# A hybrid mLSTM and sparse attention layer on one core: x laid out columns first by the host, bias tables from the host, three weight pairs multiplied part by part, two key transposes moved

## The reference

```
h = x * rsqrt(mean(x * x) + eps) * norm_gain          # first RMSNorm
proj = h @ w_in                                       # 4096 x 15416
ck, cv, sk, sv, wk, wv, a_q, gates, m_q, m_k, ... = split(proj)
k_cmp = compress(blocks of ck + cmp_k_pos), v_cmp likewise    # 15 blocks of 32 tokens
logits = q . k * scale + rel_bias[bucket(t - s)]      # compressed, selected and window keys
o = sigmoid(gates) combination of three softmax branches, times silu(a_z)
y_m = chunkwise mLSTM of conv(m_q, m_k), normed, gated
out = rmsnorm(x + concat(y_m, y_a) @ w_out)
```

## Time and profile before

| what | value |
|---|---|
| time, median of 3 runs (lowest to highest) | 1852.78 us (1850.45 to 1853.86) |
| the profiled execution: its own time, its span | 1850.58 us, 1848.8 us |
| TensorE busy, share of the span | 1820.6 us, 98% |
| VectorE, ScalarE, GpSimd busy | 62%, 45%, 4% |
| bytes moved, mean rate | 345.62 MB, 187 GB/s |
| chain that ended last, TensorE's share | 95% |

### The profile page before, as it was taken

How to read it: one execution, slowest core, us unless ns; L and a number is a source line. 1 busy time by engine, 2 the same in 40 slices (tenths; PEclk the granted TensorE clock), 3 DMA queues, 4 the chain that set the end, 5 groups by cost and what they waited for, 6 DMA issues and landing times.

```text
span 1848.8 us, 24131 instructions
## 1 busy us (share of the span) xinstructions
PE 1820.6 (98%) x8488; PEld 1511.8 (82%) x8488; DVE 1141.1 (62%) x1461; ACT 828.7 (45%) x1120; POOL 77.1 (4%) x54
## 2 busy tenths in 40 slices
PE   7999999999999999999999999999999999999997
PEld 6878888888888888888888888888888888888886
DVE  4544644467676676876666666756675775455554
ACT  5534444444454444434444444444443544444443
POOL 0000000000101010010000000000000000000000
PEclk9999999999999999999999999999999999999999
DMA  7676555544545444445555556555655566666664
GB/s 266 184 198 208 194 190 192 193 160 149 181 147 171 158 159 160 152 167 172 193 193 188 177 193 193 185 181 194 192 184 181 172 217 237 205 205 204 205 203 172
DMA packets 100266, 345.62 MB, mean 187 GB/s; under 512 B 10932, under 2 KB 16052, under 8 KB 100052
## 3 DMA queue, kind: packets, MB, share of 16 engines
q1 hardware_dynamic: 93448, 332.68, 54.1%
q10 hardware_dynamic: 6736, 11.77, 2.6%
HBM read 337.07 MB, written 7.33 MB: 186 GB/s over the span
## 4 chain that ended last, share of the span: by engine, by line
PE 95%; DMA 2%; ACT 1%; DVE 1%; issue 0%; SPq 0%; POOL 0%; ACTq 0%; DVEq 0%; POOLq 0%
PE acc_a L441 15%; PE acc_b L441 15%; PE acc_a L443 14%; PE acc_a L442 14%; PE acc_b L443 14%; PE acc_b L442 14%; PE bank_v L448 1%; DMA w_raw<-in_w_all 1%; PE bank_z L689 1%; DMA toe_dram<-toe_row 1%; PE bank_x L443 1%; PE bank_x L442 1%; PE bank_x L441 0%; ACT w_split L843 0%; PE bank_v L449 0%
## 5 line engine op out<-in xcount | busy, mean ns | idle before, releaser
L1206 DVE TENSOR_TENSOR w_split<-w_raw,w_split 128x1024 fp32r<-128x1024 f32 x620 | 777.1, 1255 | 599.2 <-ACT w_split L843 596.1
L843 ACT ACTIVATE w_split<-w_raw 128x1024 fp32r<-128x1024 f32 x620 | 655.3, 1059 | 848.9 <-PE acc_a L443 415.2
L441 PE MATMUL acc_a<-w_split,lhs_hi 128*128 128x512 f32 x1216 | 483.3, 397 | 3.2 <-DVE lhs_lo L1275 3.2
L441 PE MATMUL acc_b<-w_split,lhs_hi 128*128 128x512 f32 x1216 | 479.4, 394 | 0.3 <-issue 0.3
L443 PE MATMUL acc_a<-w_split,lhs_lo 128*128 128x512 f32 x1216 | 474.7, 390 | 0.0
L442 PE MATMUL acc_a<-w_split,lhs_hi 128*128 128x512 f32 x1216 | 474.6, 390 | 0.0
L443 PE MATMUL acc_b<-w_split,lhs_lo 128*128 128x512 f32 x1216 | 473.7, 390 | 0.0
L442 PE MATMUL acc_b<-w_split,lhs_hi 128*128 128x512 f32 x1216 | 473.6, 389 | 0.0
L441 PEld LDWEIGHTS acc_a<-w_split,lhs_hi 128*128 128x128 f32 x1216 | 229.0, 188 | 49.2 <-DVE lhs_lo L1275 2.4
L443 PEld LDWEIGHTS acc_a<-w_split,lhs_lo 128*128 128x128 f32 x1216 | 228.7, 188 | 48.7
L443 PEld LDWEIGHTS acc_b<-w_split,lhs_lo 128*128 128x128 f32 x1216 | 228.3, 188 | 48.1
(11 more groups left out here) (274 smaller groups left out, 927.0 us busy)
## 6 DMA issues: line engine op xcount, KB each, us to landing
w_raw<-in_w_all SPq DMA_DIRECT2D x616, 512.0 KB
wide<-in_x SPq DMA_DIRECT2D x8, 512.0 KB, 10.1
xres<-in_x ACTq DMA_DIRECT2D x8, 512.0 KB, 4.3
out_y<-wide SPq DMA_DIRECT2D x8, 512.0 KB, 3.2
toe_dram<-toe_row ACTq DMA_DIRECT2D x4, 766.0 KB, 10.2
toe<-toe_dram ACTq DMA_DIRECT2D x4, 512.0 KB, 4.6
gain_f<-in_final_norm_gain ACTq DMA_DIRECT2D x1, 2048.0 KB, 14.2
w_raw<-in_w_all SPq DMA_DIRECT2D x4, 224.0 KB
```

The lines of the kernel that those rows point to most:

```text
L441: pe.matmul(dst, a[0], b[0], start=start, stop=False)
L843: act.activation(w_hi[:, cols], w_raw[:, cols], ACT.Copy).then_inc(hi_done, 1)
L1206: dve.tensor_tensor(w_lo[:, cols], w_raw[:, cols], w_hi[:, cols].bitcast(F32), ALU.subtract).then_inc(lo_done, 1)
```

## The change

The host adds three arrays and drops the small ones: `x_cols_first` (x transposed, 128 partitions x (32 gains + 32 x 256 values)), `consts` (identity, masks, gains, positions, conv weights, second compressor layer, gate biases and the finished compressed bias table, 128x1318) and `toe_bias` (the finished causal bias table, 128x4096).

- SP loads `x_cols_first` in eight pieces into the memory of `lhs_lo` (`gained_x`), the first with the gains at its head, in between the first weight pairs. Weight pair 0 comes in two halves. Behind pair 7 comes `consts`, and behind each of pairs 8 to 15 an eighth of x in natural layout, which only the squares need.
- ScalarE and VectorE split x from SBUF (`first_hi`, `first_lo`), VectorE in place; the gains' transpose, `x_t`, `prepare_rows` and `prepare_bias` are gone from TensorE. The eight squares move from every second slot of block 0 to its last eight slots.
- TensorE first multiplies a tile of ones eight times (`WARM`), then pairs 0, 1 and 2 part by part (`early_pair`): hi x hi as soon as the hi parts are there, then lo of x, then lo of w.
- `copies_out` and `first_bias` are gone; ScalarE loads `toe` straight from `toe_bias` after block 0, and later groups likewise.
- T_CK moves from slot 1 to slot 6 of block 1, T_CV from the border to behind the first wide pair of block 2. T_SK moves from slot 1 to slot 2 of block 3. The parts of these transposes on ScalarE and VectorE move with them.

```diff
+WARM = 8
+XT_CHUNKS = ((0, 2), (2, 4), (4, 6), (6, 8), (8, 12), (12, 16), (16, 24), (24, 32))
...
+        gain_start = (nc.sbuf_base + 31) // 32 * 32
+        lhs_lo_start = gain_start + 4 * KT_IN
+        sb("lhs_lo_space", KT_IN + KT_IN * T)
+        gained_x = nc.alloc_sbuf_tensor_at("gained_x", [P, KT_IN + KT_IN * T], F32,
+                                           offset=gain_start)[:, :]
+        gain_t, x_t = gained_x[:, 0:KT_IN], gained_x[:, KT_IN:].rearrange("p (k t) -> p k t", t=T)
+        lhs_lo = nc.alloc_sbuf_tensor_at("lhs_lo", [P, KT_IN * T], F32R, offset=lhs_lo_start)[
+            :, :].rearrange("p (k t) -> p k t", t=T)
...
+            def fetch_xt(i):
+                if i == 0:
+                    sp.dma_start(gained_x[:, 0:KT_IN + 2 * T], x_cols_first[:, 0:KT_IN + 2 * T]
+                                 ).then_inc(xt_in[i], 16)
+                    return
+                ks = slice(*XT_CHUNKS[i])
+                sp.dma_start(x_t[:, ks, :], x_cols_first[:, KT_IN:].rearrange(
+                    "p (k t) -> p k t", t=T)[:, ks, :]).then_inc(xt_in[i], 16)
...
-            fetch_x(0)
-            fetch_first(0)
-            fetch_x(1)
+            fetch_xt(0)
+            sp.dma_start(slot_of(0, 0, 1), w_all[0:P, 0:BW]).then_inc(half_in, 16)
+            sp.dma_start(slot_of(0, 1, 1), w_all[0:P, BW:2 * BW]
+                         ).then_inc(w_loaded[0], LOADED)
+            fetch_xt(1)
             fetch_first(1)
-            fetch_x(2)
+            fetch_xt(2)
             fetch_first(2)
-            fetch_x(3)
+            fetch_xt(3)
             fetch_first(3)
-            for i in range(4, 8):
+            fetch_xt(4)
+            fetch_xt(5)
+            fetch_first(4)
+            fetch_xt(6)
+            fetch_first(5, 6)
+            fetch_xt(7)
+            fetch_first(7)
+            sp.dma_start(c128[:, :], consts).then_inc(consts_in, 16)
+            for i in range(8):
+                fetch_first(8 + i)
                 fetch_x(i)
...
-            def x_t(c):
-
-                if c % 2 == 0:
-                    pe.wait_ge(x_in[c // 2], 16)
-                if c >= 2:
-                    pe.wait_ge(ht_lo, c - 1)
+            pe.wait_ge(warm_set, 1)
+            for _ in range(WARM):
+                pe.matmul(bv[:, :], warm[:, 0:P], warm[:, :], start=True, stop=True)
...
+                def products(k, i, j):
+                    for t in range(TT):
+                        last = pe.matmul(acc[0][t][:, :], a[k][t][i], w[k][j],
+                                         start=(c, k, i, j) == (0, 0, 0, 0), stop=False)
+                    return last
+                if c == 0:
+                    pe.wait_ge(first_x_hi, 1)
+                    pe.wait_ge(half_hi, 1)
+                    products(0, 0, 0)
+                    pe.wait_ge(ht_lo, 1)
+                    products(0, 1, 0)
+                    pe.wait_ge(half_lo, 1)
+                    products(0, 0, 1)
+                    pe.wait_ge(hi_done, 1)
+                    products(1, 0, 0)
+                    products(1, 1, 0)
+                    pe.wait_ge(lo_done, 1)
+                    products(1, 0, 1).then_inc(pe_used, 1)
+                    return
+                pe.wait_ge(ht_hi, c)
+                pe.wait_ge(hi_done, c + 1)
...
+            for c in range(LOOKAHEAD):
+                early_pair(c)
+            for c in range(LOOKAHEAD, PAIRS):
                 pe.wait_ge(ht_lo, c + 1)
                 pair(0, c, 0)
-                if c + 2 < PAIRS:
-                    x_t(c + 2)
-                if c == 6:
-                    prepare_rows()
-                if c in (8, 9):
-                    prepare_bias(c - 8)
-            pe.wait_ge(pre_dve, 2)
-            pe.wait_ge(pre_act, 2)
-            stream(1, 1, {1: [lambda: transpose_stage(T_CK, 0)]})
+            pe.wait_ge(consts_in, 16)
+            stream(1, 1, {6: [lambda: transpose_stage(T_CK, 0)]})
...
-            transpose_stage(T_CV, 1)
...
+                if c == 1:
+                    transpose_stage(T_CV, 1)
...
-            stream(3, 1, {1: [key_block], 2: [hidden_t], 7: [compressed, running_sum],
+            stream(3, 1, {2: [key_block, hidden_t], 7: [compressed, running_sum],
                           10: [a_rows], 13: [m_columns]})
...
+            def first_hi(c):
+                for i, (first, _) in enumerate(XT_CHUNKS):
+                    if first == 2 * c:
+                        act.wait_ge(xt_in[i], 16)
+                for kk in (2 * c, 2 * c + 1):
+                    last = act.activation(lhs_hi[:, kk, :], x_t[:, kk, :], ACT.Copy,
+                                          scale=gain_t[:, kk:kk + 1])
+                last.then_inc(ht_hi, 1)
...
+            act.wait_ge(half_in, 16)
+            act.activation(w_hi[:, 0:BW], w_raw[:, 0:BW], ACT.Copy).then_inc(half_hi, 1)
+            act.wait_ge(w_loaded[0], LOADED)
+            act.activation(w_hi[:, BW:2 * BW], w_raw[:, BW:2 * BW], ACT.Copy).then_inc(hi_done, 1)
+            first_hi(1)
...
                 slot(0, c)
-                if c == 6:
-                    act.wait_ge(consts_in, 16 * N_CONST)
-                    act.activation(hot_r[:, :], hot_up, ACT.Copy)
-                    act.activation(rb_split[:, 0:HEADS_A], rb[:, :], ACT.Copy
-                                   ).then_inc(rb_hi_done, 1)
-                if c == 8:
-                    act.wait_ge(pre_pe, 2)
-                    act.activation(gain_mix[:, KT_IN // 2:KT_IN], bx[:, 192:192 + KT_IN // 2],
-                                   ACT.Copy)
-                    act.activation(pos_t[:, :], bx[:, 0:2 * CMP_L], ACT.Copy)
-                    act.activation(conv_w[:, :], bx[:, 128:192], ACT.Copy).then_inc(pre_act, 1)
-                if c % 2 == 1:
-                    t, i = divmod(c // 2, 4)
+                if c >= PAIRS - 8:
+                    i, t = divmod(c - (PAIRS - 8), 2)
                     act.wait_ge(x_in[2 * i], 16)
                     act.wait_ge(x_in[2 * i + 1], 16)
                     link(act.activation(junk[:, :], x_nat[:, t, i * 1024:(i + 1) * 1024],
                                         ACT.Square, accum_out=ss8[:, t, i:i + 1]))
-            act.activation(spare[:, 1:2], gain_t[:, 0:1], ACT.Copy).then_inc(pre_act, 1)
+            act.wait_ge(consts_in, 16)
+            act.activation(spare[:, 2:3], gain_t[:, 0:1], ACT.Copy).then_inc(pre_act, 1)
             act.wait_ge(pre_pool, 1)
             take(0, 0, stage[:, 0, :])
...
-            def copies_out(i):
-
-                act.wait_ge(pre_dve, 1)
...
-                act.wait_ge(toe_out, 4 * 16)
...
+            act.dma_start(toe[:, :], toe_bias[:, 0:HPG * T]).then_inc(toe_in, 16)
...
-            stream(1, {2: [lambda: transposed(T_CK, lambda i: by_group(cin[0][0])[:, 2 * i:2 * i + 2, :])],
-                       3: [lambda: copies_out(0)], 5: [positions_hi], 6: [lambda: copies_out(1)],
-                       9: [lambda: copies_out(2)], 12: [lambda: copies_out(3)],
-                       15: [first_bias]})
+            stream(1, {7: [lambda: transposed(T_CK, lambda i: by_group(cin[0][0])[:, 2 * i:2 * i + 2, :])],
+                       10: [positions_hi]})
...
-                if j == 1:
+                if j == 4:
...
+            dve.wait_ge(xt_in[0], 16)
+            for kk in range(2):
+                last = dve.tensor_scalar(lhs_hi[:, kk, :], x_t[:, kk, :], gain_t[:, kk:kk + 1],
+                                         None, ALU.mult)
+            last.then_inc(first_x_hi, 1)
+            first_lo(0)
+            dve.wait_ge(half_hi, 1)
+            dve.tensor_tensor(w_lo[:, 0:BW], w_raw[:, 0:BW], w_hi[:, 0:BW].bitcast(F32),
+                              ALU.subtract).then_inc(half_lo, 1)
+            dve.wait_ge(hi_done, 1)
+            dve.tensor_tensor(w_lo[:, BW:2 * BW], w_raw[:, BW:2 * BW],
+                              w_hi[:, BW:2 * BW].bitcast(F32), ALU.subtract).then_inc(lo_done, 1)
+            first_lo(1)
...
+        x=x, x_cols_first=np.concatenate(
+            [norm_gain.reshape(KT_IN, P).T,
+             x[0].T.reshape(KT_IN, P, T).transpose(1, 0, 2).reshape(P, KT_IN * T)], axis=1),
+        w_all=weight_stream(*map(np.asarray, (w_in, w_out, cmp_k_w1, cmp_v_w1))), final_norm_gain=final_norm_gain,
+        consts=constants(mlstm_norm_gain, cmp_k_pos, cmp_v_pos, w_conv, cmp_k_w2, cmp_v_w2,
+                         b_igate, b_fgate, rel_bias),
```

More of the change, by code:

```diff
@@ L521, in prepare_bias @@
-            def prepare_bias(t):
-                pe.wait_ge(rb_lo_done, 1)
-                for n in range(N_CMP):
-                    start = 255 + t * P - (CMP_S * n + CMP_L - 1)
-                    last = pe.matmul((bz, bv)[t][:, 2 * n * HEADS_A:2 * (n + 1) * HEADS_A],
-                                     hot_r[:, start:start + P], rb_split[:, :],
-                                     start=True, stop=True)
-                last.then_inc(pre_pe, 1)
-            pe.wait_ge(first_in, 32)
```

(24 more changed lines are left out.)

294 lines of the change are left out of this document (116 added, 178 removed).

## The result

The changed kernel takes 1867.1 us (median of 4 runs, 1866.73 to 1868.38), the kernel before 1851.62 (4 runs, 1850.14 to 1853.86). The ratio is 1.0076, with a 95% interval of 1.0063 to 1.009: 15.5 us slower. The forecast was 1829.

A forecast was written before the change was run, and what follows sets the result against it. TensorE, busy nearly the whole span, was taken as the bound; savings of 16.6 us in block 0 and 7.0 us at the transposes sum to 23.6, so 1852.8 - 23.6 = 1829 us, range 1824 to 1836.

The forecast's parts named there:

- Nothing gives it back later: the rest is paced by TensorE: After the early savings, the remaining execution: claimed no loss there, so the summed saving of 23.6 us stays whole.
- a slow stream: Block 0 loads at 225 GB/s: block 0 ends at 85, 15 us later than before, total 1861 us; chance 2%.
- The signs that I named for being wrong: Block 0 ending before 51 or after 57 us, or a new wait appearing in blocks 1 to 3.
- Block 0: Block 0 was to end at 53.5 instead of 70.1 us, saving 16.6 us.
- The rest: Key transposes behind block 0: waits and lowered clock go, saving 0.2 + 3.7 + 1.7 + 1.4 = 7.0 us.
- First wide matmul: Start of block 0: TensorE can start at about 5.8 us instead of 10.26.
- The early products and the warming: Start of block 0: part-by-part products and warm matmuls worth almost nothing; without the stream as bound, up to 4.5 + 1.5 us.
- either edit alone would do most of it: T_CV's 3.7 us wait: removing toe copies and waiting load, or moving the transposes over 3 us later, would each mostly suffice.
- The stream: Loads in block 0: 17.0 MB at 0.39 MB per us, leading TensorE after pair 3; pair 15 lands at 47.3 us.
- The waits before pairs 4 and 5: In block 0, TensorE waits 1 to 2 us for w_split there, mostly using up the 4.5 us won at the start.
- rival 1: TensorE leads in block 0, with the stream at 0.40 or more or splits too slow: saving 26 to 27, 1826 us; 17%.
- rival 2: Block 0 stream at 0.367 or less, or SP's queue runs dry: 1832 us at 0.367, 1839 at 0.32; chance 24%.

The follow-up runs named there:

- the padded version: The changed kernel with 128 unused bytes per partition ahead of `gained_x`, nothing else different: 1827.3 us, ratio 0.9865 to the kernel before.

## Why the prediction was wrong

**The step that failed** is the last one: "Nothing gives it back later: the rest is paced by TensorE". I took the 0.227 us of the kernel before for all wide matmuls of the changed one. They take 0.2333, because the 128 bytes of gains move `lhs_lo` and `w_split` against `lhs_hi` modulo 256 bytes. Measured against the padded version, which differs in nothing else, this is 1867.1 - 1827.3 = 39.8 us. No rival held it: the only case on the slow side was a slow stream, at 2%. The signs that I named for being wrong did not show it either: block 0 ended between 51 and 57, and no new wait stands in blocks 1 to 3. They all look at waits, and none at the matmul's own distance. Nor could the trace before have priced it, since all its buffers start alike; but the declaration of `gained_x` in the diff shows that buffers move, and a span in which TensorE is busy 98% of the time makes 3% of a matmul's distance larger than any wait in it.

**What held**, read from the padded version, where the address does not disturb: 1827.3 against a forecast of 1829.
- Block 0. Forecast saving 16.6, measured 70.09 - 53.88 = 16.2 (changed kernel: 16.4).
- The rest. Own times 1850.58 - 1827.52 = 23.1, less 16.2 leaves 6.9; forecast 7.0.
- First wide matmul at 5.64 in the changed kernel, forecast 5.8.
- The early products and the warming, costed at nothing: removing both gave 1826.6 instead of 1827.3.
- T_CV: "either edit alone would do most of it" holds for the copies. With T_CV at the border the padded version takes 1827.88, and the clock does not fall. The other edit alone was not tried.
- No wait for `stage` or `hid_n` is left in the list of waits.

**Steps that were off and cancelled out.** The stream was faster than 0.39 MB per us, 409 to 422 GB/s in the changed kernel, but the first loads came later. Pair 1 waited 1.38 us until 10.05 (forecast 8.9), pair 3 ran at 15.67 (14.4), pairs 4 and 5 at 19.15 and 22.81 (18.1 and 22.2 with their splits). The waits before pairs 4 and 5 are there, 0.92 - 0.23 = 0.7 and 1.02 - 0.23 = 0.8 us, smaller than the forecast, since TensorE itself came late to them. ScalarE waits for `w_raw` at both, as forecast:

```profile
16.69 1.06 ACT L849 ACTIVATE w_split<-w_raw 128x1024 fp32r<-128x1024 f32 x1 [1.70 <-DMA w_raw<-in_w_all]
...
20.34 1.06 ACT L849 ACTIVATE w_split<-w_raw 128x1024 fp32r<-128x1024 f32 x1 [1.79 <-DMA w_raw<-in_w_all]
```

Behind pair 5 of the changed kernel TensorE leads: 11 pairs of 12 x 0.2333 are 30.8 us, and 22.81 + 30.8 = 53.6. That is rival 1's mechanism, with a slower matmul. In the padded version the two paces are about equal, and one more wait appears near 42 us. So the stream did not lead as I had it, and that block 1 begins within 0.4 us of the forecast is in part luck. The Trainium skill, HBM Reference, section Specifications (TRN2), has a core streaming alone at about 425 GB/s; the 358 that I took from DMA: Bandwidth & Descriptors for rival 2 is there the share of each core when both of a pair stream. The trace, with 409 to 422, comes near the 425.

## What to carry to other kernels

When a change adds or resizes a buffer, list the start addresses of what TensorE reads, before and after, and compare them modulo 256 bytes; in this kernel 128 bytes in front of a buffer cost 40 us, more than all the waits removed were worth, and 128 unused bytes gave it back. In a kernel that TensorE bounds, first compare the start-to-start distance of the commonest matmul in both traces, then look for waits. If a change that should win by its own trace loses, run it once with the old addresses before taking it back.

## What the runs showed of the hardware

- The distance of 128x512 fp32r matmuls depends on where their operands start in SBUF relative to each other: 0.2267 us when `lhs_hi`, `lhs_lo` and `w_split` are alike modulo 256 bytes, 0.2289 at 64 bytes apart, 0.2309 at 192, 0.2333 at 128, and 0.2311 with only `lhs_lo` 128 apart. These are the distances over 80 to 92 us. The absolute start has no effect (1850.9 to 1853.1 us at 0, 128 and 192 modulo 256), and neither has a shift by a whole 256 bytes: the padded version has `lhs_lo` and `w_split` 256 bytes on from before and the distance of before, and so has the kernel with `w_raw` alone moved, whose `w_split` is 256 bytes on. The Trainium skill, TensorE: Matmul & The Clock Gate, section "Wait — 56ns, not 53.3ns?", gives 215.7 ns for back-to-back matmuls of 512 columns when warm. No stretch here was that fast: the best 18 steps in a row, in the kernel before and in the padded version, took 0.2261 us each.
- Why this is so stays open. The trace has the load of the next stationary tile (0.19 us) beside the running matmul, so two reads of SBUF may meet, which would fit a cost that depends on their relative start. But if only that load against the running matmul counted, moving `lhs_lo` alone would lengthen one step in three. In the changed kernel with `lhs_lo` apart two in three are longer: over 80 to 92 us the step from hi x hi to hi x lo takes 0.2267 us, the one into the matmul with `lhs_lo` 0.232, the one out of it 0.234. The cost is two thirds of the full one in distance (0.0044 of 0.0066 us) and in time (26.8 of 39.8 us over the padded version). No run separates the two reads.
- The first matmuls of the program ran at 0.43 us (8.41 to 11.82 in the version without the warm matmuls, behind 7.84 us without any), while the column of the granted clock says 1.00. It is the distance of the lower level: the kernel before has it between 121.45 and 121.88, in a stretch with a granted clock of 0.50. The two rows, then the stretch with the first matmuls:

```profile
121.45 0.63 PE L442 MATMUL acc_a<-w_split,lhs_hi 128*128 128x512 f32 x1
121.88 0.63 PE L443 MATMUL acc_a<-w_split,lhs_lo 128*128 128x512 f32 x1
```

```profile
8.00:11.00 3.00, 3.00 (x8) 2.32 (x9) 2.29 (x4) 2.48 (x4) 0.00 (x0) 1.00 1.03 400
```

- Idle time of about 1 us did not lower the granted clock (1.00 behind the wait at 99.51), where 3.67 us had the earlier trace rows.
